# Expert outputs of all groups summed in PSUM, tokens gathered without a normalised copy, and a ninth slot for down weights

## The reference, cut to what matters

```python
def hierarchical_moe(h, ...):          # h = rmsnorm(x, norm2_g[l])
    p_grp = softmax(h @ w_rg + b_rg);  grp_p, grp_idx = top_k(p_grp, 1)
    in_grp = (the 8 expert logits of the chosen group)
    top_l, top_j = top_k(in_grp, 2)
    weights = grp_p * softmax(top_l)
    combine = sum(one_hot(eid, 32) * weights)
    a = einsum('td,edf->tef', h, w_g);  u = einsum('td,edf->tef', h, w_u)
    hh = silu(a) * u * combine[:, :, None]
    return einsum('tef,efd->td', hh, w_d)      # added to x
```

## Time and profile before

| what | value |
|---|---|
| median of three runs | 882.54 us |
| profiled execution, its own time | 882.23 us |
| its span | 880.4 us |
| PE busy | 817.1 us (93%) |
| DVE busy | 530.9 us (60%) |
| ACT busy | 383.5 us (44%) |
| POOL busy | 117.5 us (13%) |
| moved by DMA | 281.47 MB, mean 320 GB/s |
| layer 0 experts | about 242 to 439 us |
| layer 1 experts | about 672 to 870 us |

### The profile page before, as it was taken

How to read it: one execution, slowest core, us unless ns; L and a number is a source line. 1 busy time by engine, 2 the same in 40 slices (tenths; PEclk the granted TensorE clock), 3 DMA queues, 4 the chain that set the end, 5 groups by cost and what they waited for, 6 DMA issues and landing times.

```text
span 880.4 us, 20315 instructions
## 1 busy us (share of the span) xinstructions
PE 817.1 (93%) x8747; PEld 653.6 (74%) x8747; DVE 530.9 (60%) x1067; ACT 383.5 (44%) x653; POOL 117.5 (13%) x167
## 2 busy tenths in 40 slices
PE   7999999999999997877899999999999999986884
PEld 7898788878887775664589978887889776664552
DVE  5778798658555554423377779976666455543433
ACT  5546877545422221111275577764444222211113
POOL 2840102212000000000056001023200000000000
PEclk9999999999999999988999999999999999998988
DMA  9976454498979999999998464455987999999994
GB/s 303 389 232 182 154 165 170 144 405 338 390 292 419 417 419 419 420 421 421 400 371 307 160 206 131 157 191 227 392 354 275 416 419 418 419 418 421 420 420 165
DMA packets 64125, 281.47 MB, mean 320 GB/s; under 512 B 5120, under 2 KB 7248, under 8 KB 39712
## 3 DMA queue, kind: packets, MB, share of 16 engines
q1 hardware_dynamic: 62752, 278.45, 80.9%
q0 software_dynamic: 800, 1.40, 1.1%
q10 hardware_dynamic: 480, 0.28, 0.1%
HBM read 279.06 MB, written 1.05 MB: 318 GB/s over the span
## 4 chain that ended last, share of the span: by engine, by line
PE 71%; DMA 21%; SPq 3%; DVE 2%; ACT 2%; issue 1%; DVEq 0%; ACTq 0%
PE ps L491 15%; PE ps L493 14%; PE ps L492 14%; DMA ring<-in_w_exp_up 10%; PE ps L840 9%; DMA late<-in_w_exp_down 6%; PE ps L827 5%; PE ps L856 4%; DMA new_pair<-in_w_exp_up 3%; PE ps L939 3%; SPq L381 2%; DMA ring<-in_w_in 2%; PE ps L846 1%; PE ps L603 1%; PE ps L486 1%
## 5 line engine op out<-in xcount | busy, mean ns | idle before, releaser
L1679 DVE TENSOR_TENSOR split_lo<-ring,split_hi 128x1024 fp32r<-128x1024 f32 (+1 forms) x142 | 198.0, 1430 | 33.1 <-ACT split_hi L1160 32.0
L491 PE MATMUL ps<-split_hi,hT_hi 128*128 128x512 f32 (+2 forms) x416 | 161.4, 388 | 2.1 <-DVE hT_lo L1689 1.4
L1160 ACT ACTIVATE split_hi<-ring 128x1024 fp32r<-128x1024 f32 (+1 forms) x144 | 145.9, 1048 | 32.7 <-PE ps L493 30.5
L492 PE MATMUL ps<-split_lo,hT_hi 128*128 128x512 f32 (+2 forms) x416 | 157.4, 378 | 0.0
L493 PE MATMUL ps<-split_hi,hT_lo 128*128 128x512 f32 (+2 forms) x384 | 145.2, 378 | 0.0
L2099 DVE TENSOR_TENSOR wsT<-mb,ps 32x64 f32<-32x64 f32 x256 | 54.9, 215 | 142.2 <-ACT mb L1364 139.6
L1364 ACT ACTIVATE mb<-ps 128x64 f32<-128x64 f32 x64 | 14.3, 223 | 238.4 <-PE ps L840 238.4
L491 PEld LDWEIGHTS ps<-split_hi,hT_hi 128*128 128x128 f32 x416 | 78.2, 188 | 20.3 <-issue 4.3
L492 PEld LDWEIGHTS ps<-split_lo,hT_hi 128*128 128x128 f32 x416 | 78.3, 188 | 12.9
L493 PEld LDWEIGHTS ps<-split_hi,hT_lo 128*128 128x128 f32 x384 | 72.2, 188 | 13.2
L1583 POOL TENSOR_TENSOR idx<-idx,wt 128x128 f32<-128x128 f32 x32 | 12.1, 399 | 388.4 <-PE ps L862 306.6
(11 more groups left out here) (273 smaller groups left out, 1299.1 us busy)
## 6 DMA issues: line engine op xcount, KB each, us to landing
ring<-in_w_in SPq DMA_DIRECT2D x52, 1024.0 KB, 9.5
ring<-in_w_exp_gate SPq DMA_DIRECT2D x45, 1024.0 KB, 24.3
ring<-in_w_exp_up SPq DMA_DIRECT2D x45, 1024.0 KB, 26.0
late<-in_w_exp_down SPq DMA_DIRECT2D x38, 1024.0 KB, 26.3
ring<-in_w_exp_down SPq DMA_DIRECT2D x15, 1024.0 KB, 26.6
new_pair<-in_w_exp_gate SPq DMA_DIRECT2D x10, 1024.0 KB, 18.3
new_pair<-in_w_exp_up SPq DMA_DIRECT2D x10, 1024.0 KB, 21.0
late<-in_w_exp_gate SPq DMA_DIRECT2D x9, 1024.0 KB, 24.4
```

Of the source, the lines that this page charges most:

```text
L491: mm(dst, st[0], mv[0], start=start, stop=False, skip_group_check=True)
L492: mm(dst, st[0], mv[1], start=False, stop=False, skip_group_check=True)
L1160: A(half_view(split_hi[:, v % SPLITS, :], v), raw_half(v, l), ACT.Copy).then_inc(hi_done, 1)
L1679: V.tensor_tensor(half_view(split_lo[:, v % SPLITS, :], v), raw_half(v, l), half_view(split_hi[:, v % SPLITS, :], v).bitcast(F32), ALU.sub ...
```

## The change

1. **Sum in PSUM.** The outputs of all four groups go to the accumulator banks 7, 4, 3, 6 and stay there; `add_group` and its waits are gone. x is added to once, at the end of the layer, as before for the last group.
2. **One bank each.** With four banks taken, gate/up, the transposes of the hidden values, down, and the gather have one bank each. The loop body becomes `hid_expert(e)`, `gate_up_expert(e + 1)`, `down_expert(e)`: gate and up run one expert ahead of down. The gather of the next group is cut in two halves, in the first and second expert of a group.
3. **Gather from the tokens.** The copy on ACT (line 1355) is gone. The stationary operand of the gather is `xp`, x itself read at a step of 8 elements. The scale goes into the one-hot columns: `pick_group` makes them by token tile, and a second instruction each writes them times the inverse root to `pick_ir`, which lies in `mask_c`. `mask_c` is therefore made again on GpSimd (POOL) in layer 1, and DVE waits for it (`mask_ok`).
4. **A ninth down slot** where the copy was (`merged`, the buffer `wide`). `FIRST_LOADS` gets the down of expert 9 in both layers, behind a wait for the transposes that read `wide` last (`xT_mm` 9). `NEXT_LOADS` starts with two pairs where it had four, and its lead of pairs over downs grows from 0 to 2 with e. The squares of the norm before the experts are written to `qkr`.

PE in layer 0, from the first gather on, before. `idx` holds the one-hot columns, `wide` the copy; `ring`, `new_pair`, `late` hold gate and up; `first_down` holds the down weights of expert 0.

The diff, cut to its core:

```diff
-DOWNS = (("hT1", "hT0", "lo0", "lo1", 8, "yT", "att", "br"), ("att", 8, "br", "yT", "lo0", "lo1", "hT1", "hT0"))
-RP, RD = 7, 8
+DOWNS = (("hT1", "hT0", "lo0", "lo1", 8, "yT", "att", "br", "merged"),
+         ("att", 8, "br", "yT", "lo0", "lo1", "hT1", "hT0", "merged"))
+RP, RD = 7, 9
...
-                ("u", 5), ("d", 1), ("d", 8), ("g", 6), ("u", 6), ("d", 6), ("d", 5), ("d", 3), ("g", 3), ("u", 3),
+                ("u", 5), ("d", 1), ("d", 8), ("g", 6), ("u", 6), ("d", 9), ("d", 6), ("d", 5), ("d", 3), ("g", 3), ("u", 3),
...
-NEXT_LOADS = [("gu", _e) for _e in range(RP, RD + 3)]
+NEXT_LOADS = [("gu", _e) for _e in range(RP, RD + 2)]
+_pair = RD + 2
 for _e in range(RD + 1, NE):
-    if _e + 2 < NE:
-        NEXT_LOADS.append(("gu", _e + 2))
+    _ahead = min(2, max(0, (_e - 12) // 4))
+    while _pair < min(NE, _e + _ahead + 1):
+        NEXT_LOADS.append(("gu", _pair))
+        _pair += 1
     NEXT_LOADS.append(("d", _e))
...
+        pick_ir = mask_c[:, :].rearrange("p (t s) -> p t s", t=TT)
...
-                            for c in range(4):
-                                cc = 4 * b + c
-                                for t in range(TT):
-                                    ins = mm(ps[:, b, P * c:P * c + P], wide[:, t, P * cc:P * cc + P],
-                                             pick[:, t, :], start=(t == 0), stop=(t == TT - 1),
+                    def gather_half(b, bank_no, picked=None):
+                        for t in range(TT):
+                            if picked is not None:
+                                pe.wait_ge(*picked[t])
+                            for c in range(4):
+                                ins = mm(ps[:, bank_no, P * c:P * c + P], xp[t][:, 4 * b + c, :], pick_ir[:, t, :],
+                                         start=(t == 0 and c == 0), stop=(t == TT - 1), skip_group_check=True)
...
                     for e in range(NE):
                         g, i = e // GE, e % GE
-                        if i == 0 and g + 1 < GROUPS:
-                            gather_group(g + 1)
+                        if i < 2 and g + 1 < GROUPS:
+                            gather_group_half(g + 1, i)
+                        if g >= 1 and i == (0 if g == GROUPS - 1 else 2):
+                            scatter_group(g - 1)
...
-                        if e + 2 < NE:
-                            gate_up_expert(e + 2)
+                        hid_expert(e)
                         if e + 1 < NE:
-                            hid_expert(e + 1)
+                            gate_up_expert(e + 1)
                         down_expert(e)
...
-                    act.wait_ge(inv_rms, 2 * l + 2)
-                    for t in range(TT):
-                        A(xnp[t], xp[t], ACT.Copy, scale=ir[:, t:t + 1]).then_inc(xn_act, 1)
...
+                        k = link(nc.gpsimd.memset(mask_c[:], 0.0))
+                        pool.wait_ge(pool_c, k)
+                        nc.gpsimd.affine_select(out=mask_c[:, P:], in_=mask_c[:, P:], compare_op=ALU.is_gt, fill=MASKED,
+                                                base=0, pattern=[[-1, P]], channel_multiplier=1).then_inc(mask_ok, 1)
...
+                        for t in range(TT):
+                            link(V.tensor_tensor(pick[:, t, :].rearrange("p (i s) -> p i s", i=GE),
+                                                 rankm[:, t, GE * g:GE * g + GE].rearrange("p (i o) -> p i o", o=1)
+                                                 .broadcast_to([P, GE, SLOTS]),
...
+                            V.tensor_scalar(pick_ir[:, t, :], pick[:, t, :], ir[:, t:t + 1], None, ALU.mult)\
+                                .then_inc(pick_ok, 1)
...
-                    def add_group(g, banks):
-                        for k in range(4):
-                            t, hf = k // 2, k % 2
-                            dve.wait_ge(*L(scat_mm, 4 * g + k + 1))
-                            xs = x[:, t, 512 * hf:512 * hf + 512]
-                            V.tensor_tensor(xs, xs, bank(banks[k]), ALU.add).then_inc(x_add, 1)
```

More of the change, by code:

```diff
@@ L347, in down_slot @@
                 return brf
+            if name == "merged":
+                return wide[:, :, :].rearrange("p t d -> p (t d)")
             if name in LATE_AT:
@@ L415, in build, with square_of_x @@
         spare, t2, irs = scal[:, 58:59], scal[:, 60:62], scal[:, 62:64]
-        def square_of_x(t):
-            nc.scalar.activation(wide[:, t, :], x[:, t, :], ACT.Square, accum_out=ss[:, t:t + 1]).then_inc(squares, 1)
+        def square_of_x(t, junk):
+            nc.scalar.activation(junk, x[:, t, :], ACT.Square, accum_out=ss[:, t:t + 1]).then_inc(squares, 1)
         def preload_sqrt():
@@ L461, in build @@
         xp = [x[:, t, :].rearrange("p (q c) -> p c q", c=C) for t in range(TT)]
-        xnp = [wide[:, t, :].rearrange("p (c q) -> p c q", c=C) for t in range(TT)]
         def bank(b, n=1):
@@ L924, in scatter_expert, with scatter_slots, scatter_group @@
                                     ins.then_inc(tile_mm[q], 1)
-                    def scatter_group(g, banks):
+                    def scatter_slots(y, opens):
+                        for t in range(TT):
+                            for q in range(4):
+                                ins = mm(ps[:, ACC[q], 256 * t:256 * t + 256], scatT[:, t, :],
+                                         y[:, 256 * q:256 * q + 256], start=(opens and t == 0), stop=True,
+                                         skip_group_check=True)
+                        return ins
+                    def scatter_group(g):
                         pe.wait_ge(*L(scatT_out, g + 1))
@@ L1004, in extra_pass @@
                     pe.wait_ge(x_y, 4 * n + 4)
[L1005 to L1010 removed]
+                    scatter_slots(y_slots[0], False).then_inc(x_sc, 1)
                     pe.reg_add(extra, extra, 1)
@@ L1050, in _ @@
                             sp.wait_ge(*L(pv_mm, 4))
+                        elif name == "merged":
+                            sp.wait_ge(*L(xT_mm, 9))
                         elif name == "hT1":
@@ L1228, in _ @@
                     for t in range(TT):
-                        square_of_x(t)
+                        square_of_x(t, wide[:, t, :])
                     root_of_mean(act, 2 * l)
@@ L1735, in stick_logits @@
                         dve.wait_ge(*L(zc_mm, t + 1))
+                        if t == 0 and l > 0:
+                            dve.wait_ge(mask_ok, l)
                         if t == 1:
```

266 lines of the change are left out of this document (118 added, 148 removed).

## The result

The changed kernel takes 897.61 us (897.42 to 900.01, four runs) against 882.46 us (881.25 to 882.98, four runs of before on the same chip): ratio 1.0181 with a 95% interval of 1.0164 to 1.0197, slower by 15.2 us. (The medians alone give a ratio of 1.0172.) The forecast was slower by 9.6, at 891.8, with a range up to 898. The measurement lies at that upper end: its median is just inside, and 882.54 us times 1.0181 is 898.5, just outside. The direction was right. The costs of the read and of the tail were put too low, and one step, that PE's new pace is hidden, was wrong.

A forecast was written before the change was run, and what follows sets the result against it. The prediction took the DMA queue to bound both expert stages: its start, bytes left, and PE's work behind the last landings. Terms -5.0 + 0.3 + 6.8 + 4.6 + 2.9 = +9.6 on 882.23 gave 891.8 us, range 880.5 to 898.

The forecast's parts named there:

- Part 1: Ninth down slot: expert 9's down is queued before the DMA hole, 1 MB fewer behind it, 2.5 us a layer, -5.0 us.
- Part 2: One-hot columns: four half-width DVE instructions for one start the gather 0.15 us later, +0.3 us; loss of ACT's copy gains nothing.
- Part 3: Gather from x at a 32-byte step: 0.22 us a weight load, first gather 3.4 us later per layer, +6.8 us (0 to 10.2).
- double: Gather's weight loads at 0.22 us each for 0.114, argued from ACT doubling and line 846's PE loads paying already at 8 bytes.
- Part 4: After the first release: half gathers between the first experts' gate and up leave the queue 0.65 and 1.65 us idle, +4.6 us.
- Part 5: Later groups: PE's slower pace, some 25 us a group, is hidden behind 30 us of DMA and costs nothing.
- Part 6: Tail: gate and up of expert 31 now stand behind down of 29, +1.9 us in layer 0, +1.0 us in layer 1.
- free loads: Rival: the gather's strided weight loads cost no more than loads in a row, 880.4 us; chance 0.20.
- ACT's rate on PE: Rival: the gather's weight loads take 0.27 us each, as ACT's rate at that step gives, 898.6 us; chance 0.10.
- a queue that PE's slower pace still starves after 280 us: Sign against the forecast: DMA queue in the expert stage still short of work after 280 us, putting the time above the range.

The follow-up runs named there:

- 10: Changed kernel with all gathers reading 128 neighbouring channels (other output) and eight down slots in place of nine: 893.98 us, ratio 1.0135.
- 1: Changed kernel with all gathers reading 128 neighbouring channels in place of a step of 8 elements (other output): 889.7 us, ratio 1.0093.
- 4: Changed kernel with eight down slots, the two early loads of expert 9 taken out, NEXT_LOADS starting with four pairs: 903.58 us, ratio 1.0247.
- Experiment 12: Kernel before, with the step of 32 bytes in the first gather of each layer alone: 890.29 us, ratio 1.0091.
- Experiment 11: Kernel before, with the step of 32 bytes in the gathers of groups 1 to 7 alone: 887.52 us, ratio 1.0068.
- 13: Changed kernel with all gathers reading neighbouring channels (other output) and pairs at most one ahead of downs in NEXT_LOADS: 881.26 us, ratio 0.9985.
- 14: Changed kernel with pairs at most one ahead of the downs in NEXT_LOADS, nothing else: 897.4 us, ratio 1.0182.
- 9: Changed kernel with only the gathers of groups 1 to 7 reading neighbouring channels (other output), first gathers still at the step: 897.1 us, ratio 1.0182.
- 3: Changed kernel with only the first gather of each layer reading neighbouring channels (other output): 892.64 us, ratio 1.0111.
- 8: Changed kernel with ACT's copy for the first gather alone, later half gathers in second and fourth experts, gate/up of 31 before down of 29: 894.22 us.
- experiment 2: Kernel before, with ACT's copy in x's own order and read by all gathers at a step of 8 elements: 896.81 us, ratio 1.0166.

## Why the prediction was right and wrong

- **Part 1, the slot, −5.0:** right. The load went at 220.05, and the slot measured 4.1 us in a row (10 less 1) and 6.9 at the step (4 less the changed kernel).
- **Part 2, the one-hot, +0.3:** right in kind. Line 2059's first half ended so that the loads began 0.66 us after the first instruction of `pick_group`, for 0.63 before. In layer 0 that instruction itself came 0.42 us later; why was not looked into. ACT's copy gave nothing back.
- **Part 3, the read, +6.8:** the mechanism was right, the price too low: 0.241 us a load for 0.22, 7.70 us a gather for 7.0. Experiment 12 has it alone: +8.6, where 4.05 us in each of two layers make 8.1. The reason given for "double" was half wrong (line 846), its size nearly right.
- **Part 4, the holes, +4.6:** the releases came 6.26 and 7.10 us apart for 5.65 and 6.65. With 0.241 us a load the holes are 1.26 + 2.10 a layer, 6.7 us.
- **Part 5, "Hidden": this step failed.** It set 25 us of PE's work a group against 30 us of DMA a group. The pace was right (24.75), the comparison was not. Seven pairs and ten downs are loaded or on their way when the stage begins, so the queue has to bring 25 pairs and 22 downs in it, 72 MB at 2.5 us, 180 us, while PE has to do all 32, 8 x 24.75 = 198 us. The queue is not done earlier for that, since it goes on only at 252.47, 10 us into the stage, and 10.5 us of PE's work stand behind down of 29. But PE has no slack left that could hide anything. Read as sums: PE's waits for DMA were 20.4 us in the stage, and eight gathers at 4.05 us more are 32.4 us of work. Some of the difference was paid by the clock, which PE's idle time had lowered (0.96 in the stage before, with 0.83 from 370 to 390 us, where PE was busy for 13 of 20; 1.00 after). Experiment 11 shows the step's later gathers alone at +5.9, where part 5 had 0.
- **Part 6, the tail, +2.9:** 2.8 in layer 0 and 1.2 in layer 1 from down of 29, 4.0 in all. This span was the wrong one to look at: experiment 10 shows that the order's cost begins at down of 27. But with the loads in PE's order (13) all of parts 1, 2 and 6 together measure −1.1 us, where their sum was −1.8. The lead of the pairs in `NEXT_LOADS`, which the prediction did not price at all, costs 9 us with all gathers in a row, where the queue is the bound, and nothing in the changed kernel (14).

Two accounts give the whole result. By the queue, as the prediction reckoned: down of 29 lands 11.4 us later in the two layers, where parts 1 to 4 had 6.7, and the tails are 4.0 longer, where part 6 had 2.9. Of the 4.7 us missing in the first term the price of a load explains some 3.4 (8.1 + 6.7 in place of 11.4); 1.3 stay open. By PE, which part 5 had put at nothing: experiment 14, where PE waits for no DMA, is slower by 15.0. Each bound alone leads to the same end, so that mending one of them gives back nothing (9 and 14), and 3 only half. How the loss would fall if both were mended, the later gathers in a row and the lead at one, was not run; with the first gather in a row as well, it is gone (13, −1.1 us). The step, on top of that kernel, costs 15.0 + 1.1 = 16.1 us, for which parts 3 and 4 had 11.4.

The rival "free loads" fell with the row of weight loads of line 830. "ACT's rate on PE" (0.27 us a load, 898.6) came nearest in time, by the same rule with a higher price, but it too took the pace for hidden. What the prediction named as its own undoing was "a queue that PE's slower pace still starves after 280 us". That was not it: the queue was full from 270 us on (share 1.02 at 420 to 430 in before, 1.01 now).

Open: the gaps of "issue". They are 1.2 to 5.1 us a stage in the kernels with the new order (0.4 in one stage of 8), and 0 and 2.0 us in the two stages of before, with up to 4.0 in experiment 2. In several kernels they fall at the same place of PE's program (after 38 of 64 instructions of gate and up of expert 30: 0.7 to 1.0 us). What causes them was not tested.

## What to carry to other kernels

Where a buffer is filled ahead of a stage, do not compare the paces of engine and queue: sum what each has to do from the stage's start to its end, with the queue's late start and the engine's work behind the last landing, and set added work against the sum of the engine's waits in that stage. Where both sums come out alike, mending one of them gains nothing. When an engine's order changes by one step, change the order of its loads by the same step, and look for the cost where the last long wait stands, not at the last instructions. A stationary operand of 128 float32 columns was read at a step of two floats for nearly nothing here; from four floats on it cost double.

## What the runs showed of the hardware

- A weight load of 128 float32 columns: 0.120 us apart in a row, 0.127 at a step of 8 bytes, 0.183 at 12, and 0.23 to 0.243 at every step from 16 to 32 bytes (3.84, 4.06, 5.86, and 7.38 to 7.77 us for 32 of them). These times go, roughly, by how many elements of the operand lie in 16 bytes.
- Work behind waits of PE ran at a lower clock: in experiment 10, after waits of 4.15 and 1.08 us, a scatter that takes 3.7 us elsewhere took 6.5, at a granted clock of 0.50. PE without waits ran its whole stage at 1.00, which returned part of what the longer gathers took.
